# Branch products with low parts made later, and row gathers that skip empty slots, in an encoder layer on one core

## The reference, cut to what matters

```python
h = rmsnorm(x);  x = x + mixer(h)          # two attention branches, gated
h = rmsnorm(x);  x = x + hier_moe(h)       # 4 groups of 4 experts, top-1 group, top-2 experts in it
y = rmsnorm(x)

# end of the mixer: oa, ob are the outputs of the two attention branches
gts = sigmoid(gates)
merged = gts[0] * (oa @ w_branch_a) + gts[1] * (ob @ w_branch_b)
return merged @ w_out

# experts: each is silu(t @ w_gate[e]) * (t @ w_up[e]) @ w_down[e], weighed per token
```

## Time and profile before

| | us |
|---|---|
| median of 3 executions | 894.85 (892.72 to 894.90) |
| profiled execution, device time | 895.71 |
| its span, first to last instruction | 893.90 |
| TensorE busy | 862.2 |
| VectorE busy | 459.8 |
| ScalarE busy | 391.8 |
| POOL busy | 189.0 |

### The profile page before, as it was taken

How to read it: one execution, slowest core, us unless ns; L and a number is a source line. 1 busy time by engine, 2 the same in 40 slices (tenths; PEclk the granted TensorE clock), 3 DMA queues, 4 the chain that set the end, 5 groups by cost and what they waited for, 6 DMA issues and landing times.

```text
span 893.9 us, 13782 instructions
## 1 busy us (share of the span) xinstructions
PE 862.2 (96%) x5248; PEld 729.5 (82%) x5248; DVE 459.8 (51%) x762; ACT 391.8 (44%) x555; POOL 189.0 (21%) x140
## 2 busy tenths in 40 slices
PE   7999999999999999999999999999988999899995
PEld 7988888898788888888888878888777877688863
DVE  5511356455429642324231246613688877867737
ACT  5432444454432543333334112314535667767643
POOL 2010010000100001100100000400003778777651
PEclk8999999999999999999999999999989999999999
DMA  9333132222121313231220211793879999988777
GB/s 302 105 66 96 48 77 59 66 70 56 37 70 42 95 48 64 72 90 47 35 75 17 95 48 51 223 391 128 282 254 331 364 358 381 382 302 287 255 282 299
DMA packets 97459, 141.95 MB, mean 159 GB/s; under 512 B 4720, under 2 KB 75600, under 8 KB 97392
## 3 DMA queue, kind: packets, MB, share of 16 engines
q1 hardware_dynamic: 89200, 114.50, 37.9%
q0 software_dynamic: 8176, 26.46, 10.6%
q10 hardware_dynamic: 32, 0.26, 0.3%
HBM read 116.31 MB, written 24.90 MB: 158 GB/s over the span
## 4 chain that ended last, share of the span: by engine, by line
PE 79%; DVE 6%; DMA 5%; issue 3%; ACT 3%; SPq 2%; POOL 1%; POOLq 0%; ACTq 0%; DVEq 0%
PE main L881 21%; PE main L882 20%; PE main L883 20%; PE work L967 3%; PE work L937 2%; DMA xg<-h_rows,column 2%; PE main L1001 2%; PE work L984 2%; PE work L1187 1%; PE work L954 1%; DMA e_raw<-in_w_exp_down 1%; DMA x_in<-in_x_prompt 1%; SPq L620 1%; PE work L883 1%; PE work L881 1%
## 5 line engine op out<-in xcount | busy, mean ns | idle before, releaser
L881 PE MATMUL main<-ht_hi,w_hi 128*128 128x512 f32 (+1 forms) x576 | 198.3, 344 | 0.0
L882 PE MATMUL main<-ht_lo,w_hi 128*128 128x512 f32 (+1 forms) x576 | 194.1, 337 | 0.0
L883 PE MATMUL main<-ht_hi,w_lo 128*128 128x512 f32 (+1 forms) x576 | 193.9, 337 | 0.0
L1660 DVE TENSOR_TENSOR w_lo<-raw,w_hi 128x2048 fp32r<-128x2048 f32 x29 | 66.4, 2289 | 232.5 <-ACT w_hi L1317 232.5
L881 PEld LDWEIGHTS main<-ht_hi,w_hi 128*128 128x128 f32 x576 | 109.3, 190 | 18.1 <-issue 6.6
L883 PEld LDWEIGHTS main<-ht_hi,w_lo 128*128 128x128 f32 x576 | 109.2, 190 | 11.7
L882 PEld LDWEIGHTS main<-ht_lo,w_hi 128*128 128x128 f32 x576 | 109.4, 190 | 10.7
L729 POOL DMA_DIRECT2D bias<-bias_vectors x16 | 12.3, 766 | 401.8 <-DVE nmx L1726 175.4
L881 PE MATMUL main<-w_hi,ht_hi 128*128 128x256 f32 (+1 forms) x304 | 95.9, 315 | 0.0
L883 PE MATMUL main<-w_hi,ht_lo 128*128 128x256 f32 (+1 forms) x304 | 93.1, 306 | 0.0
L882 PE MATMUL main<-w_lo,ht_hi 128*128 128x256 f32 (+1 forms) x304 | 93.1, 306 | 0.0
(11 more groups left out here) (319 smaller groups left out, 1575.5 us busy)
## 6 DMA issues: line engine op xcount, KB each, us to landing
e_raw<-in_w_exp_gate SPq DMA_DIRECT2D x16, 1024.0 KB, 8.8
e_raw<-in_w_exp_up SPq DMA_DIRECT2D x16, 1024.0 KB, 10.6
e_raw<-in_w_exp_down SPq DMA_DIRECT2D x16, 1024.0 KB, 8.3
raw<-in_w_in SPq DMA_DIRECT2D x30, 512.0 KB, 5.1
expert_rows<-y_sb SPq DMA_DIRECT2D x18, 512.0 KB, 8.3
raw<-in_w_in SPq DMA_DIRECT2D x8, 1024.0 KB, 5.4
expert_rows<-y_sb SPq DMA_DIRECT2D x1, 5632.0 KB, 22.8
raw<-in_w_out SPq DMA_DIRECT2D x4, 1024.0 KB, 6.3
```

Source lines behind the costliest of these rows:

```text
L881: pe.matmul(out, s_hi, m_hi, start=(first and i == 0), stop=False)
L882: pe.matmul(out, s_hi, m_lo, start=False, stop=False)
L883: last = pe.matmul(out, s_lo, m_hi, start=False, stop=(final and i == n - 1))
L1660: dve.tensor_tensor(w_lo[:, c % 2, :], raw[:, c % 2, :], w_hi[:, c % 2, :], ALU.subtract).then_inc(s_wlo, 1)
```

## The change

Branch products: CH_A's low part is made in two halves, after b1 and after b2 have been emptied; the low part of a merged step is made after the addition of the next step; CH_A+1's low part follows step 1 instead of step 0; ScalarE makes CH_O's high part after step 3 instead of 4. Gathers: slots without a token get the number 1024 (token numbers are written as differences to 1024, and 1024 is added at the cast), and the gather is told to leave out rows over 767.

```diff
@@ constants
+NO_TOKEN = 1024
@@ POOL, gather(r, j)
                 gp.indirect_dma_start(xg[:, j % 2, :], None, h2_dram.ap(),
-                                      bass.IndirectOffsetOnAxis(ap=ids, axis=0)).then_inc(s_xg[j % 2], 16)
+                                      bass.IndirectOffsetOnAxis(ap=ids, axis=0), bounds_check=T - 1,
+                                      oob_is_err=False).then_inc(s_xg[j % 2], 16)
@@ ScalarE, branch products
                 if j == 0:
                     split_hi(CH_A + 1)
-                if j == 4:
+                if j == 3:
                     split_hi(CH_O)
@@ VectorE, branch products
-            split_lo(CH_A)
-
+            def half_lo(c, i):
+                part = slice(1024 * i, 1024 * i + 1024)
+                dve.wait_ge(s_whi, c + 1)
+                ins = dve.tensor_tensor(w_lo[:, c % 2, part], raw[:, c % 2, part], w_hi[:, c % 2, part], ALU.subtract)
+                if i == 1:
+                    ins.then_inc(s_wlo, 1)
 
             for j in range(KD):
+                if j in (2, 3):
+                    half_lo(CH_A, j - 2)
                 n = MAIN_NO[("b", j)]
                 g = blk[:, GATE_B[j], :]
                 dve.wait_ge(s_main, n + 1)
                 dve.scalar_tensor_tensor(g, g, 1.0, main[n % 2][:, 0:T], ALU.add, ALU.mult).then_inc(s_main_v, 1)
+            def merged_lo(j):
+                dve.wait_ge(s_mhi, j + 1)
+                dve.scalar_tensor_tensor(ht_lo[:, j, :], blk[:, GATE_A[j], :], 0.5, ht_hi[:, j, :],
+                                         ALU.mult, ALU.subtract).then_inc(s_mlo, 1)
+
             for j in range(KD):
...
                 dve.tensor_tensor(g, g, gb, ALU.add).then_inc(s_merged, 1)
-                dve.wait_ge(s_mhi, j + 1)
-                dve.scalar_tensor_tensor(ht_lo[:, j, :], g, 0.5, ht_hi[:, j, :], ALU.mult, ALU.subtract).then_inc(s_mlo, 1)
-                if j == 0:
+                if j >= 1:
+                    merged_lo(j - 1)
+                if j == 1:
                     split_lo(CH_A + 1)
                 if j == 4:
                     split_lo(CH_O)
+            merged_lo(KD - 1)
             split_lo(CH_O + 1)
@@ VectorE, table of token numbers
-            dve.tensor_copy(table_u[:, :], main[1][:, 512:512 + TILES_PAD]).then_inc(s_tab, 1)
+            dve.tensor_scalar(table_u[:, :], main[1][:, 512:512 + TILES_PAD], float(NO_TOKEN), None,
+                              ALU.add).then_inc(s_tab, 1)
@@ host: constants
-    small[:, C_TOKEN:C_TOKEN + NT] = P * np.arange(NT)[None, :] + i[:, None]
+    small[:, C_TOKEN:C_TOKEN + NT] = P * np.arange(NT)[None, :] + i[:, None] - NO_TOKEN
```

## The result

The changed kernel takes 888.68 us (median of 6 runs, 886.99 to 889.29) against 894.49 of the kernel before, measured beside it. The ratio is 0.9928, with an interval of 0.9907 to 0.995. The forecast was 889.3. A repetition, reported among the experiments, gave 889.55 against 894.85, ratio 0.994 [0.9917, 0.9964]. The profiled execution took 889.29 us with a span of 887.5, against 895.71 and 893.9.

A forecast was written before the change was run, and what follows sets the result against it. TensorE, busy 96% of the span, was taken as the bound, so gains come from its idle or lower-clock time. 895.71 - 2.78 (branch products) - 2.9 (gathers) = 890.0 profiled, 889.3 as median; range 885.5 to 894.

The forecast's parts named there:

- The branch products: Stage of the branch products: TensorE's gaps before b2 and a7 vanish, 2.78 us off, bounds 0.9 and 2.8.
- the halves: CH_A's low part in two 1.23 us halves fits between b steps; the gap before b2 goes, 1.80 us.
- The gathers: Loop over expert tiles: skipping 896 empty slots of 2432 takes 2.9 us off, between 0 and 9.6.
- The shorter landing at tile 6: Wait for gather 6: 73 empty slots of 128 save 0.78 us, or 0 if the fullest DMA engine keeps its rows.
- The clock kept behind a shorter gap: After tile 6's wait: a gap of 1.1 us instead of 1.86 should keep the clock at 1.00, 1.6 us more.
- Tile 9's gap: Wait of 0.50 us at tile 9, below the 0.96 us of 90 empty slots, so all 0.50 goes.
- Tile 12, "I take 0": Wait of 3.04 us at tile 12: all slots full, lateness from weights; 3.6 us of fewer bytes offset, gain 0.
- what would show it: Signs in the loop: some 900 fewer packets, gather 6 landing about 0.8 us shorter, wait near 1.1, then clock 1.00.
- the first rival: Skipped rows help nothing: engines serving low partitions keep their rows, or descriptors stay but empty; 892.1 us, chance 0.28.
- the fixed map of partitions to DMA engines: In the gathers: each partition's row belongs to a fixed DMA engine, so landings stay; would give 892.1, not 889.3.
- The second: Rival: DMA relief removes all three waits and both lower-clock stretches of the loop, 9.6 us; 882.5 us, chance 0.12.
- The third: Rival: the bound check lengthens each gather on POOL, deciding from 0.63 us a gather; 902.5 us, chance 0.15.

The follow-up runs named there:

- e1: The kernel before with the branch products' edits alone, whole gathers kept: 891.7 us against 894.14, ratio 0.9964.
- e5: The kernel before with only CH_A's low part in two halves behind b1 and b2, whole gathers kept: 892.18 us against 893.7, ratio 0.9984.
- e13: The changed kernel with each expert's tokens dealt out over the partitions by a loaded permuted constant, same rows skipped: 888.85 us against 894.85 of the kernel before, ratio 0.9939.

## Why the prediction was right

**The branch products: right in place and size.** 2.78 us were forecast; alone they measured 2.44, and the halves 1.52 of the 1.80. Both waits vanished, the halves fitted between the steps, and nothing that was moved past came late.

**The gathers: the sum was right, its terms were not, so the sum owes something to luck.** 2.9 were forecast. The loop became 1.2 to 3.3 us shorter; the whole kernel gained 1.4 with the gathers alone and 891.7 - 888.68 = 3.0 on top of the branch part (2.2 by the repetition), values that the intervals don't separate.
- *The shorter landing at tile 6, 0.78.* Mis-sized: 0.2 in the landing, 0.12 in the wait. In the crowded stretch landings are no shorter beyond the spread between executions. The step let a gather land earlier by its own bytes; with full DMA engines it takes 8.1 us in the median even when nearly no bytes are fetched. The low bound, 0, was the better end, and "The greater part of the 8.4 is not bytes" was right.
- *The clock kept behind a shorter gap, 1.6.* Tile 6 did keep it: 9.69 us instead of 10.95, so 1.26. But the reason failed, and skipping can't be credited with it: with whole gathers e1 and e5 keep 1.00 at tile 6 as well (9.43 and 9.75 us, after gaps of 0.82 and 0.53). The changed kernel keeps 1.00 after gaps of 1.74 and 2.13, and the repetition after 2.77 us, where the transposes took 1.09. The kernel with the gathers alone had a gap of 2.74 in the same place, after which they took 1.97. The length of the gap doesn't decide it. What does stays open.
- *Tile 9's gap, 0.50.* It is 0.42 now: 0.08 instead of 0.50.
- *Tile 12, "I take 0".* With skipping the wait stays at tile 12 in two of three executions (2.77 and 2.74 us); in the third it stands at tile 13, where tile 11 is 3.4 us shorter and tile 12 1.4 longer. What the step lacked is what places a wait: a column copy of POOL that gets behind VectorE's low parts, at a tile that changes from execution to execution. The prediction had the figure for the whole stretch in the same line, "1.38 MB less is 3.6 us earlier at 384 GB/s", and set it aside because the tiles ahead would ask earlier. With that alone the loop would have been 3.7 us shorter by the rate measured here; it was 1.2 to 3.3. So the bytes of the stretch are an upper figure here, and that they are the cause is argued and not shown. How the gain divides over the tiles stays open.

Its "what would show it" missed accordingly: packets weren't fewer by 900, and the landing of gather 6 wasn't shorter by 0.8. Both had been named as signs of the first rival.

**The rivals.** The first, that skipped rows help nothing, had its premises borne out: the packets are kept, the crowded landings unchanged. Its conclusion fell: the gathers alone gain 1.4 us with an interval that leaves out nothing gained (0.6 to 3.9), and the three loops with skipping are shorter than the three with whole gathers. On the fixed map of partitions to DMA engines, which the prediction cited from the Trainium skill (DMA: Bandwidth & Descriptors, The descriptor swizzle), the idle gather speaks for it (3.2 against 2.7 us by place alone), and so may the shorter waits of e13, but nothing in the times does. The second, the whole 9.6 us, was out of reach: fetching no row at all takes 9.1 out of the loop. The third, a bound check that costs 0.63 us a gather or more, fell to 0.05 in the instruction and 0.06 ahead of it.

## What to carry to other kernels

Where the DMA engines are full over several tiles, take the bytes of the whole stretch over its rate as an upper estimate of what a change in traffic gives (1.2 to 3.3 of 3.7 us here), and expect the wait to turn up at another tile. Landing times of single transfers say little there. One trace of a loop like this is not enough to price a wait in it: executions of one kernel, and kernels that differ elsewhere, moved it by tiles and the loop by 1.6 us. Where VectorE has time to spare but TensorE waits for it, look at what stands ahead in its row: an operation that nobody needs yet, behind a wait of its own, costs a gap that moving or halving it removes. Before moving work between VectorE and POOL, look whether the times of its neighbours already depend on who starts first.

## What the runs showed of the hardware

- A row whose index is beyond the bound keeps its packet: 97459 packets in all three kernels, with 4720, 5616 and 7150 under 512 B for whole gathers, 896 and 2430 rows skipped.
- The bound check costs POOL about 0.05 us for 128 rows.
- In the crowded stretch a small POOL copy takes 0.18 to 0.20 us, and 2.2 to 2.3 when it begins inside a low part that VectorE is making; a gather's instruction takes about 1.0 or 2.2 to 3.1 in the same way. VectorE can be held up too: by 4.3 us behind an operation of POOL of 4.65.
- With the DMA engines full (a share of 1.05), a gather lands in 8.7 us in the median with a third of its rows skipped, and in 8.1 with nearly all of them skipped.
- After waits of 2.74 and 2.77 us at the same tile, one execution lost the clock (0.79 and 0.87 granted in 775 to 780 and 780 to 785) and another kept 1.00.
